# A gather queue that fetches expert rows and their coefficients: two more pairs of coefficients asked for early

## What is computed

```python
def peer_ffn(h, w_q, sk1, sk2, eu, ev):
    ...                       # per token: 8 heads x 16 best of 128 x 128 experts -> eidx, softmax g
    def chunk(args):
        ht, it, gt = args
        u = eu[it]
        a = jax.nn.gelu(jnp.einsum('ckd,cd->ck', u, ht).astype(jnp.float32), approximate=False) * gt
        return jnp.einsum('ck,ckd->cd', a.astype(ht.dtype), ev[it])
```

## Time and profile before

| | |
|---|---|
| median of 3 runs | 1506.41 us (1503.56 to 1509.64) |
| profiled execution, its time | 1507.71 us |
| profiled execution, its span | 1505.9 us |
| TensorE busy | 1476.7 us, 98% of the span |
| VectorE busy | 1329.0 us, 88% |
| GpSimd busy | 1028.0 us, 68% |
| second pass | from about 765 to 1492 us |

### The profile page before, as it was taken

One profiled execution on the slowest core, in us unless ns is written; L12 is line 12 of the kernel. 1 busy time (PEld: TensorE's weight loads), 2 busy tenths in 40 slices (PEclk: granted clock), 3 DMA queues, 4 the chain that ended last, 5 costly groups with the idle time before them and its releaser, 6 DMA issues.

```text
span 1505.9 us, 21868 instructions
## 1 busy us (share of the span) xinstructions
PE 1476.7 (98%) x7296; PEld 1234.8 (82%) x7296; DVE 1329.0 (88%) x2227; ACT 764.7 (51%) x1188; POOL 1028.0 (68%) x740
## 2 busy tenths in 40 slices
PE   7999999999999999999999999999999999999997
PEld 5887778888887888888888888888888888888886
DVE  5497666687999999979979999999999999999997
ACT  4644432433545555554554545555555555555553
POOL 6643224333787777778867777777777777777776
PEclk8999999899999999999999999999999999999999
DMA  9335447222676898989979999999999999999995
GB/s 363 103 106 175 155 154 252 84 84 85 195 238 212 267 306 260 311 263 305 316 266 390 381 397 397 391 403 399 397 396 396 394 398 395 393 402 400 391 398 193
DMA packets 219582, 444.58 MB, mean 295 GB/s; under 512 B 22360, under 2 KB 128984, under 8 KB 219232
## 3 DMA queue, kind: packets, MB, share of 16 engines
q1 hardware_dynamic: 174432, 309.04, 57.9%
q0 software_dynamic: 45056, 134.38, 23.4%
HBM read 407.68 MB, written 35.67 MB: 294 GB/s over the span
## 4 chain that ended last, share of the span: by engine, by line
PE 82%; DVE 7%; POOL 4%; DMA 3%; issue 2%; DVEq 2%; ACT 1%; POOLq 0%; SPq 0%; ACTq 0%
PE ps L1842 13%; PE ps L1815 7%; PE ps L1851 7%; PE ps L1818 7%; PE ps L1821 7%; PE ps L1767 6%; PE ps L1768 6%; PE ps L1769 6%; PE ps L1516 4%; PE ps L1518 4%; PE ps L1517 4%; PE ps L1781 2%; POOL coef L690 2%; DMA ada<-w_ada 2%; POOL rows L684 1%
## 5 line engine op out<-in xcount | busy, mean ns | idle before, releaser
L641 POOL TENSOR_TENSOR wlo<-raw,whi 128x1024 fp32r<-128x1024 f32 x178 | 428.6, 2422 | 292.5 <-ACT whi L723 291.6
L690 POOL DMA_INDIRECT coef<-gelu_spill,coef_at x256 | 320.2, 1251 | 82.8 <-issue 78.0
L684 POOL DMA_INDIRECT rows<-w_stream,row_at x256 | 245.8, 960 | 77.9 <-issue 77.6
L723 ACT ACTIVATE whi<-raw 128x1024 fp32r<-128x1024 f32 x176 | 186.2, 1060 | 144.3 <-PE ps L1769 101.9
L1842 PE MATMUL ps<-acts,whi 128*128 128x512 f32 x1024 | 253.1, 389 | 0.0
L1842 PEld LDWEIGHTS ps<-acts,whi 128*128 128x128 f32 x1024 | 192.1, 188 | 40.5
L1767 PE MATMUL ps<-whi,acts 128*128 128x512 f32 x512 | 200.1, 391 | 1.9 <-ACT gout L895 1.9
L1768 PE MATMUL ps<-wlo,acts 128*128 128x512 f32 x512 | 199.6, 390 | 0.0
L1769 PE MATMUL ps<-whi,acts 128*128 128x512 f32 x512 | 199.2, 389 | 0.0
L1455 DVE SCALAR_TENSOR_TENSOR ps<-rows,coef,ps 128x1024 f32<-128x1024 f32 x126 | 162.4, 1289 | 11.2 <-issue 0.9
L953 ACT ACTIVATE phi<-prod 128x256 fp32r<-128x256 f32 x128 | 53.5, 418 | 226.5 <-DVE prod L1426 226.5
(11 more groups left out here) (252 smaller groups left out, 2587.7 us busy)
## 6 DMA issues: line engine op xcount, KB each, us to landing
raw<-w_stream SPq DMA_DIRECT2D x304, 512.0 KB, 5.6
values_in<-w_stream SPq DMA_DIRECT2D x128, 512.0 KB, 7.7
ada<-w_ada SPq DMA_DIRECT2D x32, 512.0 KB, 4.5
gelu_spill<-gout SPq DMA_DIRECT2D x64, 256.0 KB, 5.2
gate_spill<-gblock SPq DMA_DIRECT2D x8, 2048.0 KB, 10.6
gates<-gate_spill SPq DMA_DIRECT2D x32, 512.0 KB, 8.5
ada<-w_ada SPq DMA_DIRECT2D x32, 256.0 KB, 7.2
rows<-w_stream,row_at POOLq DMA_INDIRECT x256, 6.6
```

What stands on the lines that cost most here:

```text
L641: g.tensor_tensor(wlo[:, s, :], raw[:, s, :], whi[:, s, :].bitcast(F32), ALU.subtract)\
L684: g.indirect_dma_start(rows[m % ROWS][:, :], None, w_front.rearrange("c p n -> (c p) n"), bass.IndirectOffsetOnAxis(row_at[:, t * P + n:t ...
L690: g.indirect_dma_start(coef[:, t, n:n + 1], None, gelu_dram.rearrange("t p g (e o) -> (t p g e) o", o=1), bass.IndirectOffsetOnAxis(coef_a ...
```

## The change

Two chunks are named, 6 and 10. Behind their rows GpSimd asks for two pairs of coefficients in place of one. From then on the coefficients that stand behind the rows of chunk n are those of chunk n + 2 (n = 6 to 9) and n + 3 (n from 10), up to the last, which stand behind the rows of chunk 124; the rows of 125, 126 and 127 have none behind them. The number of DMAs, their sizes and every wait stay the same. With the new line at the top all later lines of the file stand one lower, and L684 and L690 become L685 and L691.

```diff
 FIRST_ROWS = 2
 FIRST_COEFS = 3
+MORE_COEFS = (6, 10)
 COEF_RING = 8
...
+            def coefs_asked(n):
+                return min(NK, n + 1 + FIRST_COEFS - FIRST_ROWS + sum(m <= n for m in MORE_COEFS))
+
             for n in range(FIRST_ROWS, NK):
                 fetch_rows(n)
-                if n + FIRST_COEFS - FIRST_ROWS < NK:
-                    fetch_coefs(n + FIRST_COEFS - FIRST_ROWS)
+                for m in range(coefs_asked(n - 1), coefs_asked(n)):
+                    fetch_coefs(m)
```

## The result

The changed kernel takes 1514.91 us, median of 8 runs (1509.60 to 1519.71), where the kernel before, run beside it, takes 1507.81 (8 runs, 1503.56 to 1513.52). The ratio is 1.0048, interval 1.0029 to 1.0067: slower by 0.3 to 0.7%, about 7 us. The forecast was 2.2 us slower, 0.15%, which lies outside the interval. So the sign was right and the size a third of what came; the measured ratio sits just inside the prediction's bound of 0.5%, with an interval on both sides of it.

The account below looks back on a forecast made before the run. TensorE was taken to bound the last 625 us, its start set by what comes ahead. VectorE's row waits of 3.7 + 1.2 us against 2.68 saved add 2.2 us to 1506.41: 1508.6 us, range 1503.0 to 1515.

Parts of the forecast that it names:

- What the change takes away: VectorE's coefficient waits of 0.71 and 1.54 us, plus 0.43 lost at 873.76, would go: 2.68 us ahead of TensorE's long stretch.
- no wait on L1439 after 800: Sign that the forecast is right: VectorE shows no wait at this line after 800 us.
- The 0.43 at 873.76: VectorE's loss of 0.43 us there, cause unnamed, counted as following from the coefficient waits and expected to go with them.
- Two pairs cost 2.8 us of lead each: GpSimd's rows start 2.8 us later from chunk 7, 5.6 from chunk 11; lead 10.2 falls to 7.4, then 4.6.
- Taken as none: Row waits at chunks 7 to 10: lead 7.4 us against median landing 6.5; a slow row could cost up to 0.9.
- GpSimd tied to VectorE, the lead in notches: GpSimd keeps VectorE's phase at four DMAs a step; lead moves by 1.4 us, and lost lead returns only when VectorE waits.
- Chunk 11: one wait of 3.7 us: With 4.6 us of lead, VectorE waits for chunk 11's rows A, landing in 8.3 us; bounds from 1.9 us.
- Chunks 12 and 13 cost 1.2, then the notch of 8.8 covers nearly every row: VectorE's further row waits there, 0.9 to 1.2 us, taken as 1.2, until a lead of 8.8 covers nearly every row A.
- rival 2: Lead settles at 7.4 us, VectorE's waits are taken back again and again; 3 to 8 us slower, 1509.5 to 1514.5; chance 0.15.
- The sum: VectorE loses 3.7 + 1.2 = 4.9 us where it lost 2.68: 2.2 us more, all ahead of TensorE's long stretch.
- the trap at 6.0: Lead stops at 6.0 us, VectorE waits 0.5 us every step; up to 54 us slower, 1560 us; chance 0.1.
- rival 1: Stalls go and nothing replaces them, as GpSimd makes up the 5.6 us; net -2.3 us, 1504.1; chance 0.15.

Follow-up runs that it names:

- the untied kernel: Kernel before, with the low parts of u and of the values and the adding of rows B taking their second operand from PSUM; 1526.73 us, one run.
- three pairs: Changed kernel with one more pair of coefficients asked for at chunk 14; 1522.81 us, ratio 1.0090 to the kernel before.
- the one with the pause: Changed kernel in which VectorE makes the low part of the values of chunk 14 three times more; 1513.82 us, ratio 1.0036 to the kernel before.
- the late pairs: Changed kernel with its two pairs asked for at chunks 60 and 64 instead of 6 and 10; 1516.63 us, ratio 1.0058 to the kernel before.

## Why the prediction was wrong in size

- **What the change takes away**: the two waits went, the 2.68 us did not. The waits at chunks 8 and 12 are in no kernel that asks for more coefficients at chunk 6, but chunk 4's, which the change does not move, cost 1.21 (801.19 us) in after, against the sign "no wait on L1439 after 800". The 0.43 at 873.76 was no bill of the slip: a pause of 0.42 or 0.43 us stands at chunk 16 in after too (872.84), and in all eleven profiled executions in which VectorE's own list is that of before. In all, VectorE's waits for coefficients went from 4.1 to 2.4 us, where two other executions of before's list had 2.1 and 1.7.
- **Two pairs cost 2.8 us of lead each**: right. Lead 8.0 and 7.4 at chunks 7 to 10 against 7.4, 5.1 at chunk 11 against 4.6. "Taken as none" for the rows of 7 to 10 was one wait of 0.75 at chunk 7 (818.91 us), inside the bound of 0.9.
- **GpSimd tied to VectorE, the lead in notches**: right, and the untied kernel shows it. The notches seen over all runs are 7.4, 8.9/9.1, 10.1/10.35, 11.4/11.6 and 12.9/13.1.
- **Chunk 11: one wait of 3.7 us**: 0.59 and 1.00. The landing was taken from DMAs of before that started at the same moment behind another list; after's rows A landed in 5.1 us, and rows B, which were to ask for less, in 7.9 and cost the more. Four executions of the same list up to there waited 0.6, 1.0, 1.6 (three pairs) and 3.5 us (the one with the pause, whose list to chunk 11 is the same). So 3.7 is possible, and a number of the single execution.
- **Chunks 12 and 13 cost 1.2, then the notch of 8.8 covers nearly every row**: this is the step that failed. It let the first large wait carry the lead over 8 at once. As the first waits were small, the lead rose from 5.1 to 7.4 only, and there it stayed for 100 chunks: a row that lands in 7.5 to 8.1 costs VectorE less than a notch, and GpSimd's next DMAs beside VectorE are longer by as much (1.42 to 1.74). The prediction took the landings as one heap with a median of 6.5 and left open which rows come late; at this lead they are the rows A of every fourth chunk, behind the gate load, so the wait comes back with the period of the loop. This is rival 2, which had 0.15 and a price of 3 to 8 us. Its price was near, with 7 us in the timed runs and 8.0 in the 111 steps; its mechanism is the one in the trace. I had seen it at work at 831.14 and counted it for one wait, not for each one to come.
- **The sum**: VectorE was to lose 4.9 us for 2.68. It lost 14.7, of which 2.8 ahead of 860 and 12.0 behind, less 3.0 of slack, for 1.7 less of coefficient waits. To this come 2.0 us at the end, where the last rows are VectorE's, which had no term. That the sign came out right is therefore weak support for the sum: its gain and its loss were both of the wrong size.
- **The other rivals**: the trap at 6.0 did not hold; the lead was there for a dozen chunks of after and left, and the three pairs, which fell to 5.5 and 5.8, rest at 7.4 too. Stalls gone and nothing in place happens with one pair (0.9995), for another reason than rival 1's: GpSimd makes up nothing, the lead is just still enough. The Trainium skill's rule under rival 1 (Perfetto Trace Analysis, section DMA Instruction — SWDGE (GPSIMD)), that such DMAs do not read a tensor, does not fit these indirect ones: beside the same VectorE instructions with an operand in PSUM they take 0.95 us, beside those with two in SBUF mostly 1.2 to 1.7. The Trainium skill's rule in SBUF — State Buffer, section Who interferes with whom, is the one that the untied kernel bears out.

**Open.** Whether the gate load is what holds the lead at 7.4, and what lets an execution leave it; why the profiled passes of the changed kernel are 9.6 and 10.6 us longer than before's where the timed runs say 7.1 (4.4 to 10.1); why the timed cost of the late pairs (0.58%) and of the third pair is larger than their waits for rows explain.

## What to carry to other kernels

Before anything is asked for earlier in a queue that a second engine paces, count the lead of what stands behind it, in slots a step, and compare what is left with the slow landings, not with the median: four coefficient DMAs of 1.25 to 1.5 us each, asked for earlier, cost 7 us because 10.2 us of lead became 5.1 and then 7.4, and two of them, which left 8.9, cost nothing. Look for what else is loaded in the same beat, too: the slow landings came once in four chunks, beside a load that comes once in four steps. Prefer a place where the queue waits anyway (here the wait for the spill) to fill it further ahead, but mind what must follow at once: one chunk more there raised the lead to 12.9 and may have won 0.1%, two made VectorE wait 6.8 us for the first coefficients. And a wait that is shorter than a slot of the tied engine is not one payment; price it as many times as it can come back.

## What the runs showed of the hardware

GpSimd's indirect DMA takes 0.94 us of its engine, but mostly 1.2 to 1.7 where VectorE runs the low part of u or the adding of rows B, 128x1024 instructions with both large operands in SBUF, and then ends 0.82 or 0.83 us after it; with one operand in PSUM it takes 0.95 in the median. This made two engines, neither of which waited for the other's semaphore in the kernel before from 860 us on, keep step for some 110 steps, with leads that differ by 1.2 to 1.5 us and nothing between for long. A coefficient DMA of 128 x 1 values, asked for behind the rows of four chunks, landed after 10.6 us.
